# Hybrid HGRN2 and pooling backbone on one core: the later conditioning's matrix-vector product moves from TensorE to VectorE

## The reference

```python
def _adaln(cond, w, b):
    mod = jax.nn.silu(cond) @ w + b
    return jnp.split(mod[:, None, :], 3, axis=-1)
...
for i in range(DEPTH):
    shift, scale, gate = _adaln(c, ada_w[i], ada_b[i])
    hx = rmsnorm(x, norm_w[i]) * (1.0 + scale) + shift
    ...
        x = x + gate * hgrn2_mixer(hx, hgrn_w_in[j], lbs[j], hgrn_gnorm_w[j], hgrn_w_out[j], s_f, s_b)
    ...
        x = x + gate * pool_mixer(hx, rows, GRID_W, pool_w_in[j], pool_w_grp[j], pool_scale[j], pool_w_out[j])
```

## Time and profile before

| | us |
|---|---|
| runs, median of 3 | 2307.4 (2304.13 to 2309.95) |
| the profiled execution | 2312.02 |
| its span, first to last instruction | 2309.8 |
| TensorE matmul busy | 2186.8 |
| VectorE busy | 1330.0 |
| ScalarE busy | 864.7 |
| GpSimd busy | 460.8 |

### The profile page before, as it was taken

How to read it: one execution, slowest core, us unless ns; L and a number is a source line. 1 busy time by engine, 2 the same in 40 slices (tenths; PEclk the granted TensorE clock), 3 DMA queues, 4 the chain that set the end, 5 groups by cost and what they waited for, 6 DMA issues and landing times.

```text
span 2309.8 us, 34092 instructions
## 1 busy us (share of the span) xinstructions
PE 2186.8 (95%) x12258; PEld 1588.1 (69%) x12258; DVE 1330.0 (58%) x2357; ACT 864.7 (37%) x1888; POOL 460.8 (20%) x439
## 2 busy tenths in 40 slices
PE   5799999999999999999999999989999999998998
PEld 2577777677777777777777777767766666665675
DVE  6747547538638627727727727755554446464444
ACT  5744344334434424424424424444431221314222
POOL 2021221222222222212213222000034222200100
PEclk7999999999999999999999999999999999999999
DMA  6210110010010011010011011243321211113443
GB/s 254 90 42 25 35 39 28 31 44 29 27 46 31 27 44 33 22 46 27 25 42 33 28 38 32 81 151 137 137 71 42 69 42 37 51 46 122 147 137 119
DMA packets 106775, 144.80 MB, mean 63 GB/s; under 512 B 7136, under 2 KB 74224, under 8 KB 105584
## 3 DMA queue, kind: packets, MB, share of 16 engines
q1 hardware_dynamic: 99648, 125.72, 16.8%
q10 hardware_dynamic: 6960, 16.80, 1.9%
HBM read 108.91 MB, written 33.57 MB: 62 GB/s over the span
## 4 chain that ended last, share of the span: by engine, by line
PE 75%; DVE 9%; issue 8%; ACT 5%; DMA 1%; POOL 1%; SPq 0%; DVEq 0%; POOLq 0%; ACTq 0%
PE bank L1211 21%; PE bank L1212 20%; PE bank L1216 19%; PE bank L1342 3%; PE bank L1337 2%; PE bank L1457 2%; DVE w_st L1040 2%; PE bank L1357 2%; PE bank L1368 1%; PE bank L1310 1%; DVE xa L997 1%; ACT xb L667 1%; DVE qp L981 1%; DMA ada_sb<-in_ada_w 1%; ACT xb L681 1%
## 5 line engine op out<-in xcount | busy, mean ns | idle before, releaser
L1211 PE MATMUL bank<-h_hi,w_hi 128*128 128x512 f32 (+1 forms) x1472 | 569.6, 392 | 9.5 <-issue 9.5
L1212 PE MATMUL bank<-h_hi,w_lo 128*128 128x512 f32 (+1 forms) x1472 | 550.5, 379 | 6.1 <-issue 6.1
L1216 PE MATMUL bank<-h_lo,w_bf 128*128 128x512 bf16 (+1 forms) x1472 | 331.0, 368 | 0.0
L1211 PEld LDWEIGHTS bank<-h_hi,w_hi 128*128 128x128 f32 x1472 | 279.8, 190 | 64.4 <-issue 17.3
L1212 PEld LDWEIGHTS bank<-h_hi,w_lo 128*128 128x128 f32 x1472 | 279.9, 190 | 45.8
L1216 PEld LDWEIGHTS bank<-h_lo,w_bf 128*128 128x128 bf16 x1472 | 129.9, 98 | 158.5 <-issue 41.9
L649 ACT ACTIVATE xa<-bank 128x512 f32<-128x512 f32 (+1 forms) x144 | 82.6, 574 | 384.7 <-PE bank L1216 384.7
L1211 PE MATMUL bank<-wo_hi,og_hi 128*128 128x512 f32 x512 | 207.0, 404 | 12.0 <-DVE wo_lo L1086 7.9
L1040 DVE SCALAR_TENSOR_TENSOR w_st<-w_st,cv,bank 128x128 f32<-128x128 f32 x560 | 193.5, 346 | 19.0
L1212 PE MATMUL bank<-wo_hi,og_lo 128*128 128x512 f32 x512 | 201.8, 394 | 0.0
L555 POOL TENSOR_TENSOR q<-qp,cv 128x512 f32<-128x512 f32 x64 | 79.0, 1234 | 580.0 <-PE bank L1342 332.6
(11 more groups left out here) (163 smaller groups left out, 3711.3 us busy)
## 6 DMA issues: line engine op xcount, KB each, us to landing
w_raw<-in_w_in SPq DMA_DIRECT2D x80, 256.0 KB, 2.8
ada<-in_ada_late SPq DMA_DIRECT2D x128, 128.0 KB, 2.0
ada_sb<-in_ada_w SPq DMA_DIRECT2D x8, 1024.0 KB, 12.6
xt<-in_x SPq DMA_DIRECT2D x16, 512.0 KB, 5.9
gated_scratch<-o_t ACTq DMA_DIRECT2D x32, 256.0 KB, 2.4
og<-gated_scratch SPq DMA_DIRECT2D x16, 512.0 KB, 4.1
xr<-in_x SPq DMA_DIRECT2D x16, 512.0 KB, 4.8
x_scratch<-xr ACTq DMA_DIRECT2D x16, 512.0 KB, 2.6
```

The lines of the kernel that those rows point to most:

```text
L1211: pe.matmul(out_ap, hi, m_hi, start=start, stop=False)
L1212: pe.matmul(out_ap, lo, m_hi, start=False, stop=False)
L1216: return pe.matmul(out_ap, bf, m_lo, start=False, stop=stop)
```

## The change

The later conditioning's product goes to VectorE. A piece is now 128 rows of W by 256 of its columns, and one head forms 512 of the 4096 results over all 1024 rows: eight pieces (k = 0 to 7) are multiplied by silu(c) of their rows, a number per partition, and added up in a new tile `lacc`, for each of two halves. After eight pieces TensorE sums `lacc` over the partitions, with a column of ones (`one_col`), into two columns of bank MB. Sixteen pieces a head as before, with the same bytes.

`late_index` puts them at two places of a step: one at the step's top and one at its end. In heads 1 to 7 the end of step 1 has piece 0, then come top and end of steps 2 to 8, and piece 15 stands at the top of step 9. In head 0 all is three steps later: from the end of step 4 to the top of step 12. TensorE's sums stand in steps 5 and 9 (head 0: 8 and 12), right behind the projection. `ada1` stays one buffer: SP's load of a piece now waits for VectorE's count of passes (`late_acc`). VectorE adds four columns to `late` at step 14. Other edits: `reset` becomes uint8, and the squares' junk tile is one instead of two, with a wait on the square before it.

```diff
+def late_index(st, first, top):
+    i = 2 * (st - (4 if first else 1)) - (1 if top else 0)
+    return i if 0 <= i < NLATE else None
+def late_sum_at(st, first):
+    return {8: 0, 12: 1}.get(st) if first else {5: 0, 9: 1}.get(st)
+LATE_ADD = 14
+LATE_OUT = 18
...
-        reset = place("reset", [P, BLK], BF16)
+        reset = place("reset", [P, BLK], U8)
+        one_col = place("one_col", [P, 1], FP32)
...
-        junkh = place("junkh", [P, 2, P], BF16)
+        junkh = place("junkh", [P, P], BF16)
...
+        lacc = place("lacc", [P, LCOL], FP32)
...
             def load_late(h, i):
-                need(sp, "late_mm", NLATE, h, i)
-                sp.dma_start(ada1[:, :], ada_late[bass.ds(h, 1), i, :, :].rearrange("a p n -> (a p) n")
+                need(sp, "late_acc", NLATE, h, i)
+                sp.dma_start(ada1[:, :], ada_late[i % KT, bass.ds(h * 2 + i // KT, 1), :, :].rearrange("a p n -> (a p) n")
                              ).then_inc(s["late_in"], 16)
...
-                    if L0 <= st + 1 < L0 + NLATE:
-                        load_late(h, st + 1 - L0)
+                    for i in (late_index(st, first, False), late_index(st + 1, first, True)):
+                        if i is not None:
+                            load_late(h, i)
...
-                            if j >= 2:
-                                need(act, "sq_ready", 4 * NBLK, h, 4 * bi + j - 1)
-                            act.activation(junkh[:, j % 2, :], o_t[:, b, j * P:(j + 1) * P], ACT.Square,
+                            if j >= 1:
+                                need(act, "sq_ready", 4 * NBLK, h, 4 * bi + j)
+                            act.activation(junkh[:, :], o_t[:, b, j * P:(j + 1) * P], ACT.Square,
...
-                    if st == L0 + NLATE:
-                        need(dve, "late_mm", NLATE, h, NLATE)
+                    late_piece(h, late_index(st, first, True))
+                    if st == LATE_ADD:
+                        need(dve, "late_mm", 2, h, 2)
                         need(dve, "late_sum", 1, h, 1)
-                        dve.tensor_tensor(late[:, :], late[:, :], bank[MB][:, 0:4 * KT], ALU.add
-                                          ).then_inc(s["late_sum"], 1)
+                        cols = late[:, bass.ds(h * 4, 4)]
+                        dve.tensor_tensor(cols, cols, bank[MB][:, 0:4], ALU.add).then_inc(s["late_sum"], 1)
...
                     if st >= F0 + 11:
                         gate_out(h, st - (F0 + 11))
+                    late_piece(h, late_index(st, first, False))
+            def late_piece(h, i):
+                if i is None:
+                    return
+                k = i % KT
+                need(dve, "late_in", 16 * NLATE, h, 16 * (i + 1))
+                if k == 0:
+                    need(dve, "late_mm", 2, h, i // KT)
+                    dve.tensor_scalar(lacc[:, :], ada1[:, :], head_tab[:, k, 4:5], None, ALU.mult
+                                      ).then_inc(s["late_acc"], 1)
+                else:
+                    need(dve, "late_acc", NLATE, h, i)
+                    dve.scalar_tensor_tensor(lacc[:, :], ada1[:, :], head_tab[:, k, 4:5], lacc[:, :],
+                                             ALU.mult, ALU.add).then_inc(s["late_acc"], 1)
...
-                    if L0 <= st < L0 + NLATE:
-                        i = st - L0
-                        if i == 0:
-                            need(pe, "head_vec", 2, h, 1)
+                    if late_sum_at(st, first) is not None:
+                        half = late_sum_at(st, first)
+                        if half == 0:
                             need(pe, "og_ready", NBLK, h, 0)
-                        need(pe, "late_in", 16 * NLATE, h, 16 * (i + 1))
-                        for j in range(LCOL // P):
-                            c = i * (LCOL // P) + j
-                            last = pe.matmul(bank[MB][:, c:c + 1], ada1[:, j * P:(j + 1) * P], hv[:, 4:5],
-                                             start=(c == 0), stop=True, skip_group_check=True)
+                        need(pe, "late_acc", NLATE, h, KT * (half + 1))
+                        for j in range(2):
+                            last = pe.matmul(bank[MB][:, 2 * half + j:2 * half + j + 1], lacc[:, j * P:(j + 1) * P],
+                                             one_col[:, :], start=(half == 0 and j == 0), stop=True,
+                                             skip_group_check=True)
```

More of the change, by code:

```diff
@@ L690, in head @@
                                        ACT.Copy).then_inc(s["kt_ready"], 1)
-                    if last and st == 20:
+                    if last and st == 21:
                         act.wait_ge(s["late_row"], 1)
```

10 lines of the change are left out of this document (6 added, 4 removed).

## The result

The changed kernel takes 2338.9 us (median of 4 runs, 2337.07 to 2341.38) against 2308.7 for the kernel before (4 runs, 2304.13 to 2311.7): ratio 1.0132, 95% interval 1.0117 to 1.0147. It is slower by 30 us; 2345 was predicted, with a range of 2318 to 2366.

A forecast was written before the change was run, and what follows sets the result against it. TensorE, busy 95% of the span, was taken as the bound. Seven middle heads at +3.75 us (26.3) and head 0 at +11.3 on 2312.0 gave 2349.6, or 2345 on the median base; range 2318 to 2366.

The forecast's parts named there:

- TensorE's saving: 14 of 16 late blocks a head leave TensorE, 0.47 us each: 4.1 a middle head, 2.8 of it before step 9.
- The passes: Sixteen VectorE passes over 128x256 a head: 14 at 0.42 us and 2 at 0.29, 6.5 us a head.
- The round trip and the sum in step 9: Each load's round trip holds VectorE 2.33 us; the second sum makes TensorE wait 5.3; projection 11 comes 2.08 later.
- The clock: One more half-clock stretch of TensorE a head, in projection 10 after the 5.3 us wait: +2.5 us.
- Head 0: First head, pieces three steps later: wait of 2.3 us at step 8, piece pairs around VectorE's busiest stretch; +11.3 with clock.
- Small edits: Shared junk tile, uint8 reset mask, four-column add and shifted weight loads: hidden or taken as 0 us.
- Steps 14 to 17: Steps 15 to 17 end 0.83 us earlier a middle head rather than 1.41; savings in steps 11 to 14 worth nothing.
- The expected longer wait at step 14: TensorE's wait for the state chain at step 14 grows to 4 to 5 us, from 2.72.
- The head border: Steps 0 and 1 of a head: no term in the sum; half clock might catch it in the worse rival (chance 0.12, 2369).

The follow-up runs named there:

- blocks_back: two_early with ten blocks of two 128x1 matmuls per head put back on TensorE, sums not used: 2290.0 us, ratio 0.9930.
- keep_warm: Changed kernel with 20 unread matmuls on TensorE before the wait of the second sum in heads 1 to 7: 2317.0 us, ratio 1.0042.
- two_early: Changed kernel with two piece buffers and pieces one step earlier in heads 1 to 7, sums still at steps 5 and 9: 2265.4 us, ratio 0.9830.
- all_early: two_early with head 0's pieces one step earlier too: 2264.4 us, ratio 0.9815.
- small_edits: Kernel before with only the uint8 mask, the one junk tile and the added column memset: 2309.4 us, ratio 0.9998.
- sum_later: Changed kernel with the second sum of heads 1 to 7 in step 12 instead of step 9: 2308.0 us, ratio 1.0000.
- early10: Changed kernel, one buffer, heads 1 to 7 with pieces one step earlier (steps 0 to 8) and second sum at step 10: 2306.9 us, ratio 1.0001.
- early_both: early10 with head 0's pieces in steps 3 to 11 and its second sum at step 13: 2301.0 us, ratio 0.9979.
- no_late: Kernel before with one 1-column matmul in place of each step's late block, sum not used, loads and waits kept: 2283.4 us, ratio 0.9901.

## Why the prediction was right

**TensorE's saving: right.** Steps 2 to 8 lost 19.6 us, as summed; steps 11 to 13 gave nothing, and blocks_back shows the same price from the other side.

**The passes: mis-sized.** 0.48 (and 0.35 for the first of a half) instead of 0.42 and 0.29 from the nearest rows.

**The round trip and the sum in step 9: right in mechanism.** Between two passes that a load parts VectorE was idle 2.32 to 2.36 us (R was put at 2.33). The q product of projection 8 ended at S+5.46 (predicted: S+4.93), the pass behind it at S+5.93 (S+5.38), the last pass at S+8.74 (S+8.13); the wait was 5.66 instead of 5.3, and step 10 started at S+9.67 instead of S+8.6. Of these 1.07, 0.6 are the later last pass, and most of that comes from a row that the prediction had not allowed for, the first pass of the second half in step 6 of head 5 (GpSimd's cuts of the weights run from 1023.30 to 1029.61):

```profile
1028.40 1.36 DVE L1086 TENSOR_SCALAR lacc<-ada,head_tab 128x256 f32<-128x256 f32 x1
```

It took 1.36 us in heads 2 to 7, where the first pass of a half otherwise takes 0.35. The clamp of projection 6 then came 2.5 us after its step's end, and from there each step added 0.24 to 0.27 (predicted: 0.33). The other 0.5 is the sum itself, which took 0.87 until step 10 instead of 0.4: its granted clock was 0.50, right behind the wait. This term and the clock's make the +4.5 us in the balance (predicted: 8.6 + 5.39 + 2.5 less 9.11, in seven heads).

**The clock: right.** The half clock was priced at 2.5 a head. Step 10 took 6.7 to 8.05 us, 2.2 in the mean over the 5.29 that it has at full clock, and with the slow sum 2.7, which is what keep_warm took away.

**Head 0: right in size.** +9.6 against +11.3. The wait for the eighth piece was 2.3 us, as predicted; the wait for the sixteenth, in step 12, was 9.6. That two_early and all_early still take 206.1 and 205.5 us for this head, against 205.2 before, shows that the waits for loads were not all that used up TensorE's saving there.

**Small edits: right**, by small_edits.

**Steps 14 to 17: mis-sized.** -12.2 instead of -5.8. Steps 15 to 17 gave 1.18 each head, not 0.83. Step 14 was shorter by 0.9 to 1.2 us in heads 1, 2 and 7, whose mean granted clock there was 0.87 instead of 0.75, and by up to 0.35 in the others. The expected longer wait at step 14 (4 to 5 us) didn't come: the sum over that wait is 24.8 us in both kernels. The saved time of steps 12 and 13 isn't added to it: step 13 is longer instead (9.0 for 8.66), with a wait of 0.9 for the state chain ahead of the products of keys and values (line 1393).

**The head border: missing from the sum.** The prediction named the border only as something that the half clock might catch. It gave 12 us back: the first two steps took 8.9 us in two heads and 10.1 to 12.9 in five before, and 8.9 in all seven after. Before, TensorE stood still in the middle of step 0 with nothing to wait for (the kernel before, head 5):

```profile
981.38 0.28 PE L1211 MATMUL bank<-h_hi,w_hi 128*128 128x256 f32 x1
982.75 0.28 PE L1212 MATMUL bank<-h_hi,w_lo 128*128 128x256 f32 x1 [1.09 <-issue]
```

Such a stand came in each of heads 2 to 6, 1.1 to 1.4 us long, 6.1 in all; most of the rest of the 12 is the half clock, which came on top in heads 2 and 4. Without these 12 us the changed kernel would have been nearly 2% slower.

small_edits has the five stands too and so rules out the side edits. No other variant has one: the single long borders in sum_later, keep_warm, early10, early_both and no_late (10.4 to 10.5 us) have no stand but a mean granted clock of 0.62 to 0.70 in step 0. That no_late, with the loads and waits of before, has none speaks against the loads' timing, and blocks_back, with twelve of sixteen blocks, against the number of blocks.

The trace points to TensorE's own code. Heads 2 to 6 are those that follow a jump back to the loop's start. In the kernel before, a 16 KB packet of the instruction queue (q8) starts 0.4 to 1.0 us into step 0 of each of them and has come by 1.4 to 1.9; TensorE stands from 1.8 to 2.0 until 2.9 to 3.3, and the next such packet starts at 4.0 to 4.4. In the changed kernel the first packet comes at the same place, the next not before 7.9, and TensorE doesn't stand. In no_late and blocks_back, without stands, the next one starts in most heads at 5.9 to 7.2. That fits a TensorE that runs to the end of a block of code sooner behind the jump in the kernel before and waits for the next block, so that the border depends on where the loop's start lies in its block. No run moved the code alone, so this is not shown.

So the predicted 37.6 us in the heads were 22.7: +4.5 in steps 9 and 10, -6.4 in steps 14 to 17, -12.0 at the border, -1.7 in head 0, and under 1 us elsewhere. The mechanism was right: without the border the heads stand at +34.7 for the 37.6 predicted. Part of that closeness is luck, since the dearer step 9 and the larger gain in steps 14 to 17 offset each other; and the border, the largest miss, has no part in the mechanism.

## What to carry to other kernels

Work moved to an idle engine brings its loads along, and in an in-order queue a load into a single buffer stands as a wait between two instructions, so count round trips per step (here 2.8 us for each pass of 0.48), not busy time: the same passes cost 30 us with one buffer and gained 41 with two and a step's head start. Such an engine's lateness is a debt that falls due at its first reader; moving the reader alone (sum_later) only changes who waits. And whoever moves the writer (early10) must look at what it overwrites: the tile's reader has to move along, or the writer waits for it. Put a reader at least one step behind what it reads, and count the half clock behind every wait of several us on TensorE as an item of its own.

## What the runs showed of the hardware that I had not expected

- Beside GpSimd's cuts VectorE's instructions were up to 0.9 us longer: a product 1.52 for 0.69, a pass 1.37 for 0.48, and in the changed kernel the first pass of a half 1.36 for 0.35. A moment at which VectorE's last instruction is waited for shouldn't coincide with GpSimd's work.
- A load's landing fell only from 2.1 to 1.8 us with half its bytes.
- A 1-column fp32 matmul over 1-column weights cost TensorE 0.31 us of a step, two-thirds of a block of two over 128 columns.
- TensorE stood 1.1 to 1.4 us in the middle of a run of matmuls in the first step of a head, with no releaser in the profile, in each head behind the loop's jump, in two kernels of fourteen. A 16 KB packet of the instruction queue had come 1.2 to 1.5 us before each of these stands ended.
